# Two-layer hybrid block on one core: side-by-side copies of u, table loads placed by hand, transposes inside products, phi and key/value units exchanged

## The chip, the cores and the metric

The kernel runs on one core of one Trainium2 chip. The metric is the device time of one execution in microseconds. "Before" was run three times; one further execution was profiled, and every row below comes from that one.

## The reference

Two layers over 256 tokens of width 1024, in float32. Each layer is a feed-forward block, a token-mixing block of four mixers, a cross attention over 256 memory rows, and another feed-forward block, each with a norm in front and behind. Cut to what matters:

```python
for l in range(2):
    u = rmsnorm(h, ffn1_pre_g)
    h = h + 0.5 * rmsnorm((silu(u @ w_gate) * (u @ w_up)) @ w_down, ffn1_post_g)   # 2816 hidden
    u = rmsnorm(h, mix_pre_g)
    proj = u @ w_in                      # split into the inputs of four mixers
    y = [mla(...), nsa(...), fox(...), s5(...)]       # 4 heads of 64 each, s5: 16 groups, 64 states
    h = h + rmsnorm(group_rmsnorm(y) @ w_out, mix_post_g)
    u = rmsnorm(h, xa_pre_g); m = rmsnorm(mem, xa_mem_g)
    h = h + rmsnorm(cross_attention(u, m @ w_kv) @ w_o, xa_post_g)
    u = rmsnorm(h, ffn2_pre_g)
    h = h + 0.5 * rmsnorm(swiglu(u), ffn2_post_g)
```

s5 is a state-space recurrence over the tokens, computed in chunks of 4 tokens ("taps"). nsa attends to compressed blocks (phi is a two-layer map of key and value blocks), to selected blocks and to a window.

## The kernel before

**Units and slots.** All large weights come in units of 128 x 2048 float32 (1 MB), 98 per layer, in a fixed order. Unit u of a layer goes to slot (u + 98 l) mod 3. A slot has three buffers: raw (the DMA's target), w_hi and w_lo. `split` on ScalarE (L666) copies raw to w_hi in float32r in two halves; `split` on VectorE (L1144) writes w_lo = raw - w_hi, in two halves. ScalarE's split of a unit waits for its DMA and for unit_done of every earlier unit of the slot, since it overwrites w_hi. SyncE loads the next unit of a slot as soon as VectorE has split the last one. TensorE (PE) makes every large product three times: w_hi x_hi, w_lo x_hi, w_hi x_lo. The four phi units of a layer are the exception: PE reads them raw, they are never split, and the next load of the slot waits for PE instead.

**Order.** Each engine runs a list written out by hand and executes it in order; semaphores join the lists. PE waits in its own order, so whatever stands behind a waiting product waits too.

**Feed-forward.** 11 chunks of 256 hidden columns. `gate_up` (L1777) makes the products of one chunk for token halves t = 0 and 1 (units a and b), with the transposes of the chunk before in between; `ffn_down` follows. The first chunk, `gate_up_first` (L1802), also transposes the rows of h (`rows_of`), which ScalarE and VectorE turn into x_hi and x_lo (`fill_hi_of`, `fill_lo_of`, counted in x_split). On ScalarE the first block of a layer has two loops, chunks 2 to 4 and chunks 5 to 9; between them stand an Exp, an Abs and four Sin for the state-space tables, after which GpSimd builds these tables. In the first layer chunk 1 also holds the transposes of the scaled memory rows (`mem_transposed`, L1824), which ScalarE copies out and stores.

**Mixing.** Middle units m = 0 to 31: eight for w_in, then twelve, 8 to 19, of which 11, 13, 16, 18 are phi units and the others key/value units (KV0 to KV7) of the cross attention, then four for the output projection (20 to 23), four for queries and four for the cross attention's output. Middle unit m lies in slot m mod 3 in layer 0. PE's list from the selected-block attention (group 1) to the window attention (group 2), shortened:

```python
phi_unit(2); kv_half(6, 0); probs_transposed(1); kv_half(6, 1); phi_unit(3)
kv_half(7, 0); times_values(1)           # L2161
... # phi_t
kv_half(7, 1)                            # L2169
pe.wait_ge(*E.at("att_out", 3))
scores(2)                                # L2171
```

VectorE has `split_mid(21)`, `attention_out(1)` one behind the other (L1539, L1540), and ScalarE has `split_mid(21)`, the tanh of phi, `evac_kv(7)`, `split_mid(22)` (L1038 to L1043). The attention groups run in the order 0, 3, 1, 2; att_out 3 is the end of attention_out(1).

**State space.** u of the mixer is scaled in bank 5 of PSUM (s5_us), then copied to s_u with a rotation of its 32-partition blocks: sixteen copies of 32 x 128, eight by ScalarE (taps j = 0, 1), then eight by VectorE (taps 2, 3).

Of the kernel before, what the change touches and what calls it, by code (L numbers as in the profile page):

```python
# [9 lines left out]
ACT = mybir.ActivationFunctionType  # L10
# [6 lines left out]
KT = D // P  # L17
# [12 lines left out]
CH = 4  # L30
# [13 lines left out]

PHI_UNITS = [N_IN + i for i in (3, 5, 8, 10)]
KV_UNITS = [N_IN + i for i in (0, 1, 2, 4, 6, 7, 9, 11)]
KV_BANK = [0] + 7 * [1]
# [79 lines left out]
def program(nc, x, memory, weights, cols, mats, post, consts, out, mem_scratch):  # L127
# [5 lines left out]
    with ctx:  # L133
# [526 lines left out]
        def _(act):  # L660
            a = nc.scalar

            for l in range(DEPTH):
# [91 lines left out]
                def ffn_first(f):  # L755

                    if l == 0 and f == 0:
                        fill_hi_of(3 * f, 1, range(6))
                        split(*ffn_unit(l, f, "a", 1))
                        tanh_of(f, 0, 0)  # L760
                        fill_hi_of(3 * f, 1, (6, 7))
                        h_square(3 * f, 1)
                        load_gain(3 * f)
                        split(*ffn_unit(l, f, "b", 1))
                        tanh_of(f, 0, 1)
                        act.wait_ge(s_mem, 16)
                        for t in range(TT):
                            i = a.activation((mix_out, qk_a)[t][:, 0:D], mem3[:, t], ACT.Square, accum_out=ss[N_QM][:, t:t + 1])
                        i.then_inc(b_ss, 1)
                    else:  # L770
                        split(*ffn_unit(l, f, "a", 1))
                        fill_hi_of(3 * f, 1, range(6))
                        h_square(3 * f, 1)
                        load_gain(3 * f)
                        tanh_of(f, 0, 0)
                        fill_hi_of(3 * f, 1, (6, 7))
                        split(*ffn_unit(l, f, "b", 1))
                        tanh_of(f, 0, 1)
# [49 lines left out]
                a.activation(zone[:, 3072:3584], proj[:, 40:552], ACT.Sin, scale=-1.0, bias=quarter)  # L828
                a.activation(zone[:, 3584:4096], nsa_q[:, 40:552], ACT.Sin).then_inc(sem["trig_done"], 1)
                with act.Fori(FU // 2, FU - 1) as i:  # L830
                    ffn_piece(0, i, False)
                    act.wait_ge(s_con, 16)
# [40 lines left out]
                u_to = v3(s_u.rearrange("p g q -> p (g q)"), "p (i a q) -> p a i q", i=2, a=4)  # L873
                for j in range(2):
                    for q in range(4):
                        i = a.activation(u_to[32 * j:32 * j + 32, q], u_ps[32 * q:32 * q + 32, :, :, CH - 1 - j],
                                         ACT.Copy)
                i.then_inc(sem["proj_done"], 1)

                split_mid(4)  # L880
                evac(0, 1)
                split_mid(3)
                act.wait_ge(*E.at("s5_t", 1))
# [123 lines left out]
                evac_kv(1)  # L1007
                split_mid(12)
                act.wait_ge(*E.at("fox_cum", 1))
                for hh in range(H):  # L1010
# [12 lines left out]
                evac_kv(4)  # L1023
                split_mid(17)
                act.wait_ge(*E.at("nsa_t", 2))
                a.activation(nsa_q[0:HD, :], bank(6, 2)[0:HD], ACT.Copy).then_inc(sem["nsa_tc_act"], 1)
                evac_kv(5)
                attention(1)

                attention_t(1)  # L1030
                split_mid(19)
                evac_kv(6)
# [99 lines left out]
        def _(dve):  # L1132
            v = nc.vector

            for l in range(DEPTH):
# [120 lines left out]
                def ffn_first(f):  # L1256

                    fill_lo_of(E.at, 3 * f, 1, range(6))
                    split(*ffn_unit(l, f, "a", 1))
                    fill_lo_of(E.at, 3 * f, 1, (6, 7))  # L1260
                    gate_of(f, 0, 0)
# [42 lines left out]
                tt(u_in, u_in, row_r2, ALU.mult).then_inc(sem["s5_us"], 1)  # L1304
                dve.wait_ge(*E.at("proj_done", 2))
                u_ps = v3(bank(5), "p (i q r) -> p i q r", i=2, r=CH)
                u_to = v3(s_u.rearrange("p g q -> p (g q)"), "p (i a q) -> p a i q", i=2, a=4)
                for j in (2, 3):
                    for q in range(4):
                        i = v.tensor_copy(u_to[32 * j:32 * j + 32, q], u_ps[32 * q:32 * q + 32, :, :, CH - 1 - j])  # L1310
                i.then_inc(sem["s5_u_dve"], 1)
                dve.wait_ge(*E.at("s5_k", 1))
                tt(k_ps[:, :, 0:C2], k_ps[:, :, 0:C2], v3(pmat[:, W_D:W_D + PAIRS * C2], "p (g c) -> p g c",
                                                                g=PAIRS), ALU.add).then_inc(sem["s5_kd"], 1)
                split_mid(4)
                split_mid(3)
                dve.wait_ge(*E.at("s5_t", 1))
# [205 lines left out]
                attention_out(3)  # L1523
                split_mid(17)
                attention_max(1)

                attention_copy(1)
                split_mid(19)
                s, n, _ = mid(l, PHI_UNITS[3])
# [120 lines left out]
        def _(pe):  # L1650
# [4 lines left out]
            for l in range(DEPTH):  # L1655
# [91 lines left out]

                def gate_up_tile(f, unit, half, t, fill=None):

# [3 lines left out]
                    if not by_piece:  # L1753
                        pe.wait_ge(*E.at(split_done[s], ns + 1))
                    for k in range(KT // 2):
                        if by_piece and half == 0:
                            pe.wait_ge(*E.at(split_done[s], k - 2))
                        elif by_piece and k % 2 == 0:
                            pe.wait_ge(*E.at(split_done[s], k // 2))
# [17 lines left out]
                def gate_up(f, i):  # L1777

                    (a_, an, ans), (b_, bn, bns) = (ffn_unit(l, f, r, i) for r in ("a", "b"))
                    for t in range(TT):  # L1780
                        pe.wait_ge(*E.at("hid_done", i * 2 + (2 * f * FU + t - 1)))
                        o = gate_up_tile(f, (a_, an, ans), 0, t)
                        if t == 1:
                            o.then_inc(sem[unit_done[a_]], 1)
                        o = gate_up_tile(f, (b_, bn, bns), 1, t)
                        if t == 0:
                            o.then_inc(sem["gu_half"], 1)
                            hid_transposed(f, i - 1)
                            if l == 0 and f == 0 and isinstance(i, int) and i == 1:
                                mem_transposed()  # L1790
                    o.then_inc(sem[unit_done[b_]], 1)
# [10 lines left out]
                def gate_up_first(f):  # L1802
# [7 lines left out]
                    rows_of(p, 0, range(6, KT))  # L1810
                    gate_up_tile(f, b_, 1, 0, fill).then_inc(sem["gu_half"], 1)
                    rows_of(p, 1, range(6))
                    pe.wait_ge(*E.at("hid_done", 2 * f * FU))
                    gate_up_tile(f, a_, 0, 1, fill).then_inc(sem[unit_done[a_[0]]], 1)
                    rows_of(p, 1, range(6, KT))
                    gate_up_tile(f, b_, 1, 1, fill).then_inc(sem[unit_done[b_[0]]], 1)
# [97 lines left out]
                pe.wait_ge(*E.at("row_scale_kept", 1))  # L1914
                pe.wait_ge(s_con, 16)
                pe.wait_ge(*E.at("s5_u_dve", 1))
                for q in range(2):
# [493 lines left out]
```

## Time and profile before

| | us |
|---|---|
| three runs | 1291.06, 1292.61, 1293.25 |
| median | 1292.61 |
| profiled execution | 1290.97 |
| its span, first to last instruction | 1289.1 |
| PE busy | 1260.7 |
| VectorE busy | 820.6 |
| ScalarE busy | 668.1 |
| GpSimd busy | 236.5 |

Busy is the time in which an engine has an instruction in work. Matmuls are pipelined and their ends are modelled, so a row of PE shows when a product starts, and its drawn end overlaps the next one. The idle time in brackets counts from the drawn end. A line number can be a helper's: L1659 is every matmul, L1139 every tensor-tensor operation of VectorE. DVE is VectorE, ACT is ScalarE, POOL is GpSimd, SP is SyncE.

### The profile page before, as it was taken

What the parts mean: (1) busy time and instruction counts of PE and PEld (TensorE: products, weight loads), DVE (VectorE), ACT (ScalarE), POOL (GpSimd) and SP (SyncE); (2) the same over time, 40 slices, a digit from 0 to 9 for tenths busy, and PEclk for the clock granted to TensorE, in tenths of its full rate; (3) what the DMA queues carried; (4) which work ended last, traced back from release to release, by engine and by line L of the source; (5) the groups of instructions that cost most, each with busy time, mean ns of one, the idle gap of its engine ahead of it and who ended that gap; (6) DMA issues with size and microseconds to landing.
All of it is one profiled execution on the core that took longest, in us unless ns stands there. A gap on an engine that the chain in (4) does not pass through costs nothing.

```text
span 1289.1 us, 18528 instructions
## 1 busy us (share of the span) xinstructions
PE 1260.7 (98%) x6836; PEld 1072.6 (83%) x6836; DVE 820.6 (64%) x1155; ACT 668.1 (52%) x1091; POOL 236.5 (18%) x251
## 2 busy tenths in 40 slices
PE   7999999999999999999999999999999999999998
PEld 5888788899988878888878878888998798788886
DVE  5657956775557565555576587667856565755554
ACT  6455546574536564444464545564745455644442
POOL 1618911000002010000045297000000010100000
PEclk9999999999999999999999999999999999999999
DMA  9754554334525356555455555533245243655551
GB/s 342 256 189 153 191 195 148 135 125 146 199 84 184 127 209 220 177 184 193 164 183 193 195 176 183 180 147 140 105 164 205 90 174 128 232 179 186 176 187 65
DMA packets 32442, 222.65 MB, mean 173 GB/s; under 512 B 3584, under 2 KB 4096, under 8 KB 6784
## 3 DMA queue, kind: packets, MB, share of 16 engines
q1 hardware_dynamic: 30080, 209.28, 45.0%
q10 hardware_dynamic: 2304, 12.58, 2.6%
q8 instruction: 38, 0.62, 0.2%
q14 instruction: 20, 0.16, 0.0%
HBM read 219.75 MB, written 2.10 MB: 172 GB/s over the span
## 4 chain that ended last, share of the span: by engine, by line
PE 88%; DVE 5%; issue 3%; ACT 2%; DMA 1%; POOL 1%; SPq 0%; DVEq 0%; ACTq 0%; POOLq 0%
PE PS L1659 83%; DVE w_lo L1139 3%; PE PS L1774 1%; DMA raw<-in_weights 1%; PE PS L1988 1%; DVE x_lo L1142 1%; ACT w_hi L671 1%; DVE rope_t L1310 0%; ACT x_hi L719 0%; DVE work L1142 0%; DVE h L1142 0%; PE PS L1800 0%; PE PS L2241 0%; PE PS L1972 0%; PE PS L2032 0%
## 5 line engine op out<-in xcount | busy, mean ns | idle before, releaser
L1139 DVE TENSOR_TENSOR w_lo<-raw,w_hi 128x1024 fp32r<-128x1024 f32 (+1 forms) x378 | 484.0, 1323 | 221.2 <-ACT w_hi L671 217.7
L671 ACT ACTIVATE w_hi<-raw 128x1024 fp32r<-128x1024 f32 x368 | 368.9, 1053 | 207.8 <-PE PS L1659 203.0
L1659 PE MATMUL PS<-w_hi,x_hi 128*128 128x512 f32 (+2 forms) x1104 | 425.4, 385 | 13.5 <-DVE w_lo L1139 7.0
L1659 PE MATMUL PS<-w_lo,x_hi 128*128 128x512 f32 (+2 forms) x1104 | 413.5, 375 | 0.0
L1659 PE MATMUL PS<-w_hi,x_lo 128*128 128x512 f32 (+2 forms) x1104 | 407.7, 375 | 0.0
L1659 PEld LDWEIGHTS PS<-w_hi,x_hi 128*128 128x128 f32 x1104 | 208.3, 189 | 58.0 <-issue 10.6
L1659 PEld LDWEIGHTS PS<-w_hi,x_lo 128*128 128x128 f32 x1104 | 208.1, 189 | 38.2
L1659 PEld LDWEIGHTS PS<-w_lo,x_hi 128*128 128x128 f32 x1104 | 208.5, 189 | 34.8 <-issue 0.5
L521 POOL TENSOR_SCALAR st<-st 128x1 f32<-128x1 f32 x32 | 20.3, 634 | 619.8 <-ACT proj L694 550.8
L1659 PE MATMUL PS<-w_hi,hid_hi 128*128 128x512 f32 x336 | 131.5, 391 | 0.0
L1659 PE MATMUL PS<-w_lo,hid_hi 128*128 128x512 f32 x336 | 130.8, 389 | 0.0
L732 ACT ACTIVATE work<-PS,st 128x256 f32<-128x256 f32 x88 | 41.9, 476 | 149.1 <-PE PS L1659 147.5
L1659 PE MATMUL PS<-w_hi,hid_lo 128*128 128x512 f32 x336 | 103.5, 389 | 0.0
L1659 PE MATMUL PS<-x_hi,w_hi 128*128 128x256 f32 x288 | 84.2, 292 | 1.0 <-DVE x_lo L1142 0.9
L1142 DVE SCALAR_TENSOR_TENSOR work<-work,PS 128x256 f32<-128x256 f32 x88 | 36.5, 414 | 71.5 <-ACT work L732 71.5
L1659 PE MATMUL PS<-x_lo,w_hi 128*128 128x256 f32 x288 | 81.4, 283 | 0.0
L1659 PE MATMUL PS<-x_hi,w_lo 128*128 128x256 f32 x288 | 81.3, 282 | 0.0
L1659 PEld LDWEIGHTS PS<-w_hi,hid_lo 128*128 128x128 f32 x336 | 63.1, 188 | 13.2
L1659 PEld LDWEIGHTS PS<-w_lo,hid_hi 128*128 128x128 f32 x336 | 63.1, 188 | 12.8
L1659 PEld LDWEIGHTS PS<-w_hi,hid_hi 128*128 128x128 f32 x336 | 63.1, 188 | 12.8
L1659 PEld LDWEIGHTS PS<-x_hi,w_hi 128*128 128x128 f32 x288 | 55.0, 191 | 3.2 <-issue 2.7
L1659 PEld LDWEIGHTS PS<-x_lo,w_hi 128*128 128x128 f32 x288 | 55.1, 191 | 0.1
(274 smaller groups left out, 1334.5 us busy)
## 6 DMA issues: line engine op xcount, KB each, us to landing
raw<-in_weights SPq DMA_DIRECT2D x194, 1024.0 KB, 4.8
pmat<-in_mats ACTq DMA_DIRECT2D x3, 1664.0 KB, 7.8
gain<-in_post ACTq DMA_DIRECT2D x8, 512.0 KB, 3.7
zone<-mem_scratch ACTq DMA_DIRECT2D x2, 1024.0 KB, 5.7
raw<-in_weights SPq DMA_DIRECT2D x3, 512.0 KB, 7.3
h<-in_x SPq DMA_DIRECT2D x2, 512.0 KB, 6.2
zone<-in_mem SPq DMA_DIRECT2D x1, 1024.0 KB, 11.1
mem_scratch<-zone ACTq DMA_DIRECT2D x1, 1024.0 KB, 9.0
```

The costliest lines, as they stand in the source:

```text
L521: E.step(g.tensor_scalar(o, a, s1, s2, op0, op1))
L671: a.activation(w_hi[s][:, c_], raw[s][:, c_], ACT.Copy).then_inc(sem[hi_done[s]], 1)
L732: a.activation(f_th[:, t], bank(4 + t)[:, 0:UC], ACT.Tanh, scale=rstd[n][:, t:t + 1]).then_inc(sem["tanh_done"], 1)
L1139: return v.tensor_tensor(o, x_, y_, op)
L1142: return v.scalar_tensor_tensor(out=o, in0=x_, scalar=s_, in1=y_, op0=op0, op1=op1)
L1659: return t_.matmul(o, a_, b_, start=first, stop=last)
L1774: o = t_.transpose(bank(6)[:, j * S + t * P:j * S + (t + 1) * P], f_hid[:, t, j * P:(j + 1) * P], ident)
L1988: i = t_.transpose(bank(b)[:, hh * P:(hh + 1) * P], probs[:, at:at + P], ident)
```

## The change

- Phi and key/value units are exchanged in the load order: units 16 and 18 become KV6 and KV7, 17 and 19 phi 2 and phi 3. PE's list stays. The splits of 17 and 19 become 16 and 18, and split(18) goes ahead of attention_t(1).
- In the opening of a feed-forward block the x tiles 6 and 7 of token half 1 are filled earlier on ScalarE, in the first opening of all on VectorE too. On PE the row transposes of token half 1 stand inside the products of units a and b, not between them.
- mem_transposed moves twelve products further down in chunk 1, behind unit a's products of token half 1.
- A Tanh on one column stands ahead of ScalarE's second loop, an Exp on one column behind split(12). They place the table loads.
- Both engines copy u at the same time: ScalarE the blocks q = 0, 1 for all four taps, VectorE q = 2, 3. Units 3 and 4 are split in this order.

```diff
-PHI_UNITS = [N_IN + i for i in (3, 5, 8, 10)]
-KV_UNITS = [N_IN + i for i in (0, 1, 2, 4, 6, 7, 9, 11)]
+PHI_UNITS = [N_IN + i for i in (3, 5, 9, 11)]
+KV_UNITS = [N_IN + i for i in (0, 1, 2, 4, 6, 7, 8, 10)]
...
@@ -756,9 +756,9 @@
                         fill_hi_of(3 * f, 1, range(6))
+                        fill_hi_of(3 * f, 1, (6, 7))
                         split(*ffn_unit(l, f, "a", 1))
                         tanh_of(f, 0, 0)
-                        fill_hi_of(3 * f, 1, (6, 7))
...
@@ -827,6 +827,7 @@
                 a.activation(zone[:, 3584:4096], nsa_q[:, 40:552], ACT.Sin).then_inc(sem["trig_done"], 1)
+                a.activation(st[:, 0:1], ident[:, 0:1], ACT.Tanh)
                 with act.Fori(FU // 2, FU - 1) as i:
...
-                for j in range(2):
-                    for q in range(4):
+                for q in range(2):
+                    for j in range(CH):
                         i = a.activation(u_to[32 * j:32 * j + 32, q], u_ps[32 * q:32 * q + 32, :, :, CH - 1 - j],
                                          ACT.Copy)
                 i.then_inc(sem["proj_done"], 1)
+                split_mid(3)
+                evac(0, 1)
                 split_mid(4)
-                evac(0, 1)
-                split_mid(3)
...
                 split_mid(12)
+                a.activation(st[:, 0:1], ident[:, 0:1], ACT.Exp)
                 act.wait_ge(*E.at("fox_cum", 1))
...
-                split_mid(17)
+                split_mid(16)
...
                 attention(1)
+                split_mid(18)
                 attention_t(1)
-                split_mid(19)
                 evac_kv(6)
...
@@ -1256,8 +1258,12 @@
-                    split(*ffn_unit(l, f, "a", 1))
-                    fill_lo_of(E.at, 3 * f, 1, (6, 7))
+                    if l == 0 and f == 0:
+                        fill_lo_of(E.at, 3 * f, 1, (6, 7))
+                        split(*ffn_unit(l, f, "a", 1))
+                    else:
+                        split(*ffn_unit(l, f, "a", 1))
+                        fill_lo_of(E.at, 3 * f, 1, (6, 7))
...
-                dve.wait_ge(*E.at("proj_done", 2))
+                dve.wait_ge(*E.at("s5_us", 1))
-                for j in (2, 3):
-                    for q in range(4):
+                for q in (2, 3):
+                    for j in range(CH):
...
+                split_mid(3)
                 split_mid(4)
-                split_mid(3)
...
-                split_mid(17)
+                split_mid(16)
                 attention_max(1)
+                split_mid(18)
                 attention_copy(1)
-                split_mid(19)
...
@@ -1753,6 +1759,8 @@
                     for k in range(KT // 2):
+                        if between and k == KT // 4:
+                            between()
...
                         if t == 1:
                             o.then_inc(sem[unit_done[a_]], 1)
+                            if l == 0 and f == 0 and isinstance(i, int) and i == 1:
+                                mem_transposed()
                         o = gate_up_tile(f, (b_, bn, bns), 1, t)
                         if t == 0:
                             o.then_inc(sem["gu_half"], 1)
                             hid_transposed(f, i - 1)
-                            if l == 0 and f == 0 and isinstance(i, int) and i == 1:
-                                mem_transposed()
...
-                    gate_up_tile(f, b_, 1, 0, fill).then_inc(sem["gu_half"], 1)
-                    rows_of(p, 1, range(6))
+                    def next_rows():
+                        pe.wait_ge(*E.at("x_split", FILL[fill] + KT))
+                        rows_of(p, 1, range(6))
+
+                    gate_up_tile(f, b_, 1, 0, fill, next_rows).then_inc(sem["gu_half"], 1)
                     pe.wait_ge(*E.at("hid_done", 2 * f * FU))
-                    gate_up_tile(f, a_, 0, 1, fill).then_inc(sem[unit_done[a_[0]]], 1)
-                    rows_of(p, 1, range(6, KT))
+                    gate_up_tile(f, a_, 0, 1, fill, lambda: rows_of(p, 1, range(6, KT))).then_inc(sem[unit_done[a_[0]]], 1)
...
                 pe.wait_ge(*E.at("row_scale_kept", 1))
                 pe.wait_ge(s_con, 16)
+                pe.wait_ge(*E.at("proj_done", 2))
                 pe.wait_ge(*E.at("s5_u_dve", 1))
```

## Rows read from the trace of the kernel before

**Rows 1.** The page, part 1: busy time and share of the span, one engine.

```profile
PE 1260.7 (98%) x6836; PEld 1072.6 (83%) x6836; DVE 820.6 (64%) x1155; ACT 668.1 (52%) x1091; POOL 236.5 (18%) x251
```

**Rows 2.** The page, part 5: columns are instruction, busy, mean ns, idle before, releaser.

```profile
L1139 DVE TENSOR_TENSOR w_lo<-raw,w_hi 128x1024 fp32r<-128x1024 f32 (+1 forms) x378 | 484.0, 1323 | 221.2 <-ACT w_hi L671 217.7
...
L671 ACT ACTIVATE w_hi<-raw 128x1024 fp32r<-128x1024 f32 x368 | 368.9, 1053 | 207.8 <-PE PS L1659 203.0
```

**Rows 3.** Waits of PE: released line, releaser, us in total, times, longest.

```profile
PE PS L1723 <- DVE h L1142: 2.5, 2, 1.3
```

**Rows 4.** Timeline of the opening, ScalarE and PE: start, us, instruction, idle before.

```profile
19.59 2.01 ACT L671 ACTIVATE w_hi<-raw 128x1024 fp32r<-128x1024 f32 x2 [0.94 <-DMA raw<-in_weights]
...
23.36 0.50 PE L1659 MATMUL PS<-w_hi,x_hi 128*128 128x512 f32 x1 [0.85 <-DVE x_lo L1142]
...
32.05 1.20 PE L1829 MATMUL PS<-con,zone 128*128 128x128 f32 x9 [1.16 <-DVE zone L1269]
...
34.05 1.89 ACT L747 ACTIVATE zone<-PS 128x2048 f32<-128x2048 f32 x1 [1.77 <-PE PS L1829]
```

**Rows 5.** Timeline of the second feed-forward opening: ScalarE, VectorE, PE.

```profile
464.78 2.00 ACT L671 ACTIVATE w_hi<-raw 128x1024 fp32r<-128x1024 f32 x2
...
464.67 0.61 DVE L1142 SCALAR_TENSOR_TENSOR x_lo<-PS,pcol,x_hi 128x128 fp32r<-128x128 f32 x2 [0.42 <-ACT x_hi L719]
...
468.24 0.47 PE L1659 MATMUL PS<-w_hi,x_hi 128*128 128x512 f32 x1 [0.46 <-DVE x_lo L1142]
```

**Rows 6.** Timeline of the state-space start: ScalarE, VectorE, PE.

```profile
219.91 2.23 ACT L876 ACTIVATE rope_t<-PS 32x128 f32<-32x128 f32 x8 [2.84 <-DVE PS L1139]
...
222.17 2.41 DVE L1310 COPY rope_t<-PS 32x128 f32<-32x128 f32 x8 [2.30 <-ACT rope_t L876]
...
229.76 0.49 PE L1659 MATMUL PS<-w_hi,x_hi 128*128 128x496 f32 x1 [0.26 <-DVE w_lo L1139]
```

**Rows 7.** Timeline around the third group's exponentials: ScalarE, PE.

```profile
298.60 1.53 ACT L1011 ACTIVATE qk_a<-PS 1x256 f32<-1x256 f32 x4 [2.32 <-PE PS L1659]
...
316.80 1.28 ACT L935 ACT_TABLE_LOAD   x1
...
320.83 0.85 PE L1988 MATMUL PS<-con,zone 128*128 128x128 f32 x6 [0.62 <-ACT zone L938]
```

**Rows 8.** Timeline of the second loop, VectorE.

```profile
127.67 7.94 DVE L1139 TENSOR_TENSOR w_lo<-raw,w_hi 128x1024 fp32r<-128x1024 f32 x4
```

**Rows 9.** Chain in the second loop (start, us, what), and PE's row there.

```profile
120.80 1.07 ACT w_hi L671
...
132.44 0.50 PE L1659 MATMUL PS<-w_hi,x_hi 128*128 128x512 f32 x1 [0.80 <-DVE w_lo L1139]
```

**Rows 10.** Timeline around units 18 to 21: PE, ScalarE, VectorE, PE.

```profile
347.37 0.36 PE L1659 MATMUL PS<-w_hi,x_hi 128*128 128x256 f32 x1 [0.68 <-DVE w_lo L1139]
...
351.63 2.00 ACT L671 ACTIVATE w_hi<-raw 128x1024 fp32r<-128x1024 f32 x2 [1.21 <-DMA raw<-in_weights]
...
352.98 2.35 DVE L1139 TENSOR_TENSOR w_lo<-raw,w_hi 128x1024 fp32r<-128x1024 f32 x2
...
355.25 0.22 DVE L1445 TENSOR_SCALAR st<-PS 128x4 f32<-128x4 f32 x2
...
356.83 0.48 PE L1659 MATMUL PS<-nsa_k,nsa_q 64*128 64x256 f32 x1
```

**Rows 11.** Timeline of PE at the start.

```profile
8.72 0.76 PE L1659 MATMUL PS<-w_hi,x_hi 128*128 128x512 f32 x1 [2.32 <-DVE w_lo L1139]
...
12.67 0.39 PE L1659 MATMUL PS<-w_hi,x_hi 128*128 128x512 f32 x1
```

**Rows 12.** Windows at the end: bounds, length, busy by engine, PEclk, DMA share, GB/s.

```profile
1282.00:1284.00 2.00, 1.18 (x6) 0.64 (x4) 1.46 (x2) 1.23 (x4) 0.43 (x1) 1.00 0.00 0
...
1285.50:1286.00 0.50, 0.00 (x0) 0.00 (x0) 0.50 (x2) 0.00 (x0) 0.00 (x0) 0.80 0.96 393
...
1286.00:1289.00 3.00, 0.00 (x0) 0.00 (x0) 0.68 (x2) 0.00 (x0) 0.00 (x0) 0.50 0.47 175
```

More of the change, by code:

```diff
@@ L774, in ffn_first @@
                         load_gain(3 * f)
+                        fill_hi_of(3 * f, 1, (6, 7))
                         tanh_of(f, 0, 0)
-                        fill_hi_of(3 * f, 1, (6, 7))
                         split(*ffn_unit(l, f, "b", 1))
@@ L1746, in _, with gate_up_tile @@
                 hid_tiles = [(hid_hi[:, j * S:(j + 1) * S], hid_lo[:, j * S:(j + 1) * S]) for j in range(2)]
-                def gate_up_tile(f, unit, half, t, fill=None):
+                def gate_up_tile(f, unit, half, t, fill=None, between=None):
                     s, _, ns = unit
```

## Prediction

> **What bounds the kernel.** I read the page first. Its first part puts TensorE at 98% of the span [rows 1], and the chain of work that ended last runs through PE's three-pass products nearly all the way. So an edit gains only where PE waits, and costs only where it makes PE wait. VectorE and ScalarE have room on average, but each weight unit passes through both: two ScalarE halves of about 1.05 us and two VectorE halves of about 1.2 us [rows 2]. I then went through the timeline of PE for every place where one product starts later than the pace allows. A 512-column product starts every 0.23 us but is drawn 0.39 us long, a 256-column one every 0.12 and 0.28; so a wait costs the idle time in the bracket plus 0.16 us. The waits that the diff can touch, each read in the timeline of the engine that ends it, are few and short: they add up to some 15 us, a little over 1% of the time. After the start the longest is 1.3 us idle, in a line that the diff doesn't touch [rows 3]. A new wait of a few us would therefore weigh as much as everything that can be won.
>
> **The change, part by part.**
>
> Opening of the first feed-forward stage and the memory rows. PE waits 0.85 us for the last two x tiles of token half 1, because ScalarE and VectorE split unit a of chunk 1 first, at 19.59, the moment it lands; it waits 1.16 us for the scaled memory rows [rows 4]. With the 0.16 these are 1.01 and 1.32 us, and the first x tile of token half 1 costs another 0.55 us some 5 us earlier (0.39 idle, the pattern of rows 5). The first goes: rows 6 and 7 are transposed some 2 us sooner and filled before the split. The second goes: twelve products of 0.23 us (2.7 us) now stand in front of the memory transposes, and the ScalarE copy behind them (1.9 us [rows 4]) ends before twelve more products do. But something is late next: chunk 1 may start only when the gate of chunk 0 has emptied bank 4. That gate stands behind the split, which can't start before the landing, 19.5. Split and gate end about 24.0; PE would be there at 23.1. So 2.9 us of waits go and 0.9 us comes: gain 1.95 us, bounds 1.0 and 2.9.
>
> The other three openings (the rows of token half 1 inside the products). PE waits 0.46 us after the six transposes [rows 5], and 0.49 and 0.46 in the two others, so 0.62 each with the drawn end. Six products (1.36 us) now follow those transposes. The fill on ScalarE stands behind a split that ends at 466.8 in any case [rows 5], so the first x tile is complete at 467.6, when PE, after the same number of transposes and products, wants it. About 0.05 us each is left: gain 3 x 0.57 = 1.7 us, bounds 1.0 and 1.9. The new wait for all eight x tiles of half 0 costs nothing: the last is written at 465.3 [rows 5], the products reach it at 465.6.
>
> Copies of u. ScalarE takes 2.23 us for its eight copies and VectorE only then 2.41 us for its own [rows 6]; VectorE's splits of two units follow, unit 4 ahead of unit 3, and PE waits 0.26 us for unit 3 [rows 6], 0.42 by start times. Side by side the copies end at about 222.2. Unit 3's slot is free at about 225.1, whoever copies (PE's last products on unit 0 end then); with unit 3 first it is ready at 228.5, before PE wants it at 229.3. The next thing late is the copy of the tap tables behind unit 4's split, ending about 232.1 on VectorE, which is when PE arrives. Gain 0.4 x 2 layers = 0.8 us, bounds 0 and 0.85. That both engines read one bank at once may slow the copies; 2.8 us of slack hide it.
>
> Exp table. The load of 1.28 us stands directly ahead of the third group's exponentials, and PE waits 0.62 us for their end [rows 7], 0.78 by start times. After the split of unit 12 ScalarE is idle for 2.32 us before fox_cum [rows 7], so the load is hidden there, and the exponentials begin 0.9 us sooner. Gain 0.78 x 2 = 1.55 us, bounds 1.2 and 1.6.
>
> Table loads out of the second loop. Four loads of 1.28 us per layer, each as in [rows 7], leave ScalarE. The PE waits nearest to them are 0.96 us (0.80 idle, at 132.44 [rows 9]) and 0.78 us (17.7 us later) per layer. But those are VectorE's: the chain runs from PE's release at 120.80 over w_hi [rows 9] straight into VectorE's w_lo, whose four halves from 127.67 take 7.94 us with no idle time in front [rows 8], 2.0 each where 1.2 is usual, while GpSimd works on large state-space tables. The table load is not in this chain. I take nothing; bounds 0 and 3.4 us.
>
> Units exchanged. Before, unit 19 (KV7, slot 1) could only be loaded once phi unit 2 was used up; its split comes late and PE waits 0.68 us [rows 10], about 1.0 by start times. Now KV7 is unit 18 in slot 0; its raw data is there early, its split goes ahead of attention_t(1), and this wait is gone: gain 0.95 us per layer (the evacuation of bank 1 by ScalarE is what PE then meets).
> The price is one unit later. Slot 0 next takes unit 21, an output-projection unit. A phi unit is used raw and never occupies w_hi; KV7 does. split(21) starts at 351.63 now, released by its DMA alone [rows 10], since slot 0's last user, phi unit 3, is long done. After the change ScalarE must wait with it for the end of kv_half(7,1). That lies just behind 356.83, the start of the next product [rows 10]; 0.95 us sooner it is about 355.95. VectorE has the same split in its queue directly ahead of attention_out(1), and the PE instruction right behind kv_half(7,1) is scores(2), which waits for that attention_out [rows 10]. Step by step: ScalarE half 1.1, two VectorE halves 2.4, the six operations of attention_out(1) 1.45 (from 355.25 [rows 10] to 356.7), the semaphore 0.13: scores(2) starts at 360.9. Before the change PE passes here without a wait; it would now be ready at 355.85. That is a new wait of 5.05 us. Nothing covers it: PE executes in order, and the phi tail, mixer transposes and output rows are all behind scores(2). ScalarE and VectorE later keep their old distances to scores(2), so nothing is given back. Bounds 3.6 (should attention_out overlap) and 5.3. Net of the exchange: 10.1 - 1.9 = +8.2 us.
>
> Sum without the clock: -1.95 - 1.7 - 0.8 - 1.55 + 8.2 = +2.2 us.
>
> The clock. At the start nine 512-column products run at 0.44 us each, from 8.72 to 12.67; from there they stand 0.23 apart [rows 11]. That is the step from 1.2 to 2.4 GHz, and the slow stretch cost 9 x 0.21 = 1.9 us. At the end PE's last product ends at 1283.2; the granted clock is still 1.00 until 1285.5, 0.80 in the next half us and 0.50 after [rows 12]. So there 2.6 us of rest were enough to bring it down. The new wait is twice that. I expect it to fall in each layer and PE to work on at half pace for a while; bounds per layer 0 and 1.9 us, and because part of the slow stretch may lie in the wait itself I take 1.65, together +3.3 us.
> The Trainium skill (TensorE: Matmul & The Clock Gate, Part 1) says that an idle PE is gated back to the lower clock and gets the full one only after sustained work; the rows at both ends of this trace agree, and by that rule the sum is +5.5 us, without it +2.2.
>
> Total: +2.2 + 3.3 = +5.5 us. The profiled execution took 1290.97 us (span 1289.1 and 1.9 around it), which gives 1296.5. The median of the three runs is 1292.61, 1.64 above, so I add this: **1298 us**.
>
> **Rivals.**
> 1. The new wait without the clock: 1292.6 + 2.2 = 1294.8. For it: no wait now in the kernel brings the clock down, the longest included [rows 3]. Against: the end of the trace [rows 12]. 0.15.
> 2. The other side: the exchange does not block. Should VectorE finish the attention output before PE needs it, or the split chain be largely covered, the 7.9 us of removed waits stay: 1292.6 - 7.9 = 1284.7 with no new wait. It decides at 4.0 us of new wait per layer with the clock held (2.3 with it lost): below that the kernel is faster. Against it: queue order and slot arithmetic are fixed, and the chain's durations are all measured. 0.10.
> 3. The table loads do carry the loop's waits: 3.4 us more gain, 1294.6. For it: they stand in the same iterations. Against: VectorE has no idle time in front of the waiting product. 0.07.
> 4. More is lost: the early reordering pays nothing, a clock loss costs the full 1.9 or more, the feed-forward openings meet new waits: 1300 to 1303. 0.08.
> The forecast has 0.60.
>
> **How the numbers follow.** A difference under 0.2% (2.6 us) can't be told from none. Range: forecast with its bounds 1295 to 1300.5; rivals 1 and 3 at 1294.7 come in with their spread, rival 2 stays out: 1292.5 to 1301. Faster (below 1290.0) 0.12: rival 2 and a bit of 3. Same 0.23: rivals 1 and 3 for the most part, and the low edge of the forecast. Slower 0.65.
>
> **What would show it.** In the profile after, PE stands before the first scores product of the window group (nsa_k, nsa_q) in both layers for 5 us, released by VectorE's mix_out; w_hi of that unit starts right after the last product of kv_half(7,1), not on a DMA. The granted clock of the 10 us after each of these waits is under 1.00, and 512-column products there are 0.43 apart. ScalarE has no table load inside the loop, yet the PE waits near 132 and 150 are still there. The waits at 320.8, 347.4, 229.8 and 468.2 are gone. It is wrong if scores(2) starts within 2 us of kv_half(7,1), or if the loop waits vanish with the table loads.

## The result, and the profile after

The change made the kernel slower: 1303.85 us median of four runs (1302.3 to 1305.04) against 1291.84 of four runs of before beside them (1290.84 to 1293.25), a ratio of 1.009 with a 95% interval of 1.0074 to 1.0106. I had forecast 1298, in a range of 1292.5 to 1301: the direction was right, the size was not. The profiled execution after the change has a span of 1301.2 us, before 1289.1, so 12.1 us have to be found.

The page after, part 1, one row. PE has as many instructions as before and is drawn busy for 6.8 us longer [rows 1]: it does the same work more slowly somewhere.

```profile
PE 1267.5 (97%) x6836; PEld 1078.9 (83%) x6836; DVE 824.4 (63%) x1155; ACT 658.9 (51%) x1087; POOL 239.2 (18%) x251
```

Waits of PE after: released line, releaser, us in total, times, longest.

```profile
PE PS L1665 <- DVE mix_out L1141: 9.8, 2, 4.9
PE PS L1665 <- DVE w_lo L1141: 6.5, 5, 3.8
PE PS L1665 <- DVE x_lo L1144: 4.8, 11, 0.6
```

The first row is new: two waits of 4.9 us, one in each layer, on the attention output. Of the longest waits no other grew, except that the longest on w_lo is now 3.8 us; that one is the first, at the start (below). Here is that place in the first layer, in the timeline of the kernel after, one engine behind the other: ScalarE, VectorE, PE (start, us, instruction, idle before).

```profile
354.16 2.00 ACT L671 ACTIVATE w_hi<-raw 128x1024 fp32r<-128x1024 f32 x2 [5.79 <-PE PS L1665]
...
355.25 2.36 DVE L1141 TENSOR_TENSOR w_lo<-raw,w_hi 128x1024 fp32r<-128x1024 f32 x2 [4.25 <-ACT w_hi L671]
357.53 0.22 DVE L1451 TENSOR_SCALAR st<-PS 128x4 f32<-128x4 f32 x2
...
358.22 0.76 DVE L1141 TENSOR_TENSOR mix_out<-PS,st 128x256 f32<-128x256 f32 x2
...
353.84 0.28 PE L1665 MATMUL PS<-w_hi,x_lo 128*128 128x256 f32 x1
359.03 1.22 PE L1665 MATMUL PS<-nsa_k,nsa_q 64*128 64x256 f32 x2 [4.91 <-DVE mix_out L1141]
```

This is the chain I had worked out: PE finishes kv_half(7,1) (last product at 353.84), only then does ScalarE start w_hi of unit 21. Its bracket names PE, where before it named the DMA [rows 10]. VectorE's halves of unit 21 follow, then attention_out(1), then scores(2). By start times the wait is 359.03 - 353.84 - 0.12 = 5.07 us (forecast 5.05). In the second layer scores(2) starts at 1000.34, again with 4.91 us idle.

What I had too small comes next. Windows of the kernel after: bounds, length, busy by engine, then the granted clock (PEclk), DMA share, GB/s.

```profile
354.00:357.60 3.60, 0.12 (x2) 0.00 (x0) 2.35 (x4) 2.00 (x2) 0.00 (x0) 1.00 0.00 0
357.60:367.84 10.24, 8.81 (x34) 7.50 (x35) 7.93 (x20) 4.06 (x9) 0.00 (x0) 0.50 0.55 190
367.84:372.00 4.16, 4.16 (x27) 3.44 (x25) 1.64 (x5) 3.02 (x10) 0.00 (x0) 1.00 0.10 39
999.30:1009.54 10.24, 9.20 (x35) 7.77 (x36) 7.98 (x17) 4.45 (x10) 0.00 (x0) 0.50 0.59 205
```

The clock falls to 0.50 (1.2 GHz) inside the wait, 1.4 us before scores(2), and stays there for 10.24 us, of which PE works 8.8. To price it, take the distance from scores(2) to the transpose of h that ends PE's wait for VectorE's h; both ends are rows. After the change they are these.

```profile
402.95 1.29 PE L1729 MATMUL PS<-con,h 128*128 128x128 f32 x8 [1.24 <-DVE h L1144]
...
1044.46 1.51 PE L1729 MATMUL PS<-con,h 128*128 128x128 f32 x10 [1.24 <-DVE h L1144]
```

The distance is 402.95 - 359.03 = 43.92 us and 1044.46 - 1000.34 = 44.12 us. Before, the first was 396.71 - 356.83 = 39.88 [rows 10]. These are the rows of before that end it, and both ends in the second layer.

```profile
396.71 0.96 PE L1723 MATMUL PS<-con,h 128*128 128x128 f32 x5 [1.28 <-DVE h L1142]
...
991.93 2.88 PE L1659 MATMUL PS<-nsa_k,nsa_q 64*128 64x256 f32 x16
...
1031.76 1.51 PE L1723 MATMUL PS<-con,h 128*128 128x128 f32 x10 [1.27 <-DVE h L1142]
```

The second layer's distance was 39.83. So the slow stretches cost 4.04 and 4.29 us, 8.3 us in all, where I had put 3.3.

The smaller edits, in the timeline after: PE at the start, the loop (VectorE, PE), the copies of u and the next wait of PE, the Exp's table load.

```profile
10.01 0.77 PE L1665 MATMUL PS<-w_hi,x_hi 128*128 128x512 f32 x1 [3.79 <-DVE w_lo L1141]
...
12.71 0.47 PE L1665 MATMUL PS<-w_hi,x_hi 128*128 128x512 f32 x1
...
25.05 0.50 PE L1665 MATMUL PS<-w_hi,x_hi 128*128 128x512 f32 x1 [0.69 <-DVE work L1144]
...
126.68 7.93 DVE L1141 TENSOR_TENSOR w_lo<-raw,w_hi 128x1024 fp32r<-128x1024 f32 x4
...
131.43 0.50 PE L1665 MATMUL PS<-w_hi,x_hi 128*128 128x512 f32 x1 [0.76 <-DVE w_lo L1141]
...
218.90 2.22 ACT L877 ACTIVATE rope_t<-PS 32x128 f32<-32x128 f32 x8 [2.85 <-DVE PS L1141]
...
218.90 2.42 DVE L1316 COPY rope_t<-PS 32x128 f32<-32x128 f32 x8
...
230.78 0.39 PE L1665 MATMUL PS<-w_hi,x_lo 128*128 128x496 f32 x1
231.22 0.63 PE L1665 MATMUL PS<-rope_t,zone 128*128 128x64 f32 x4
...
295.03 1.28 ACT L1010 ACT_TABLE_LOAD   x1
```

The gate of chunk 0 is what PE meets at 25.05, 0.85 us by start times (forecast 0.9). The table load now runs at 295.03, ahead of its use. The copies of u start together, and neither engine is slowed by it although both read one bank: 2.22 and 2.42 us for eight copies, 2.23 and 2.41 before [rows 6]. The wait in the loop is still there at 131.43, with no table load near it. The start itself was 1.3 us later in this execution (first product 10.01, before 8.72 [rows 11]); ScalarE's first split there starts when the DMA of the first weights lands, at 8.55 (7.26 before), which the diff doesn't touch.

### The profile page after: what moved, and what is told of

It reads as the page before. It is cut to its first block, busy times and chain, and to the rows that moved or that the text cites. A ratio compares the mean times of both kernels' runs of the same rounds, so it can differ in the third digit from the quotient of the medians.

```text
span 1301.2 us, 18571 instructions
## 1 busy us (share of the span) xinstructions
PE 1267.5 (97%) x6836; PEld 1078.9 (83%) x6836; DVE 824.4 (63%) x1155; ACT 658.9 (51%) x1087; POOL 239.2 (18%) x251
## 4 chain that ended last, share of the span: by engine, by line
PE 91%; DVE 4%; issue 2%; ACT 1%; DMA 1%; POOL 0%; SPq 0%; ACTq 0%; DVEq 0%; POOLq 0%
PE PS L1665 86%; DVE w_lo L1141 2%; PE PS L1782 1%; PE PS L1999 1%; DVE x_lo L1144 1%; DMA raw<-in_weights 1%; ACT w_hi L671 1%; PE PS L1808 1%; DVE work L1144 0%; DVE h L1144 0%; PE PS L2050 0%; DVE mix_out L1141 0%; ACT x_hi L719 0%; PE PS L1983 0%; PE PS L1930 0%
```

## The experiments

Each ratio is against before, run beside it on the same chip: 1291.13 us for the first four, again 1291.13 on another chip for the next four, 1291.26 on a third for the last two. Between these groups, and against the 1303.85 above, the ratios compare better than the times.

**The exchange, undone and alone.** First the changed kernel without the exchange:

```diff
-PHI_UNITS = [N_IN + i for i in (3, 5, 9, 11)]
-KV_UNITS = [N_IN + i for i in (0, 1, 2, 4, 6, 7, 8, 10)]
+PHI_UNITS = [N_IN + i for i in (3, 5, 8, 10)]
+KV_UNITS = [N_IN + i for i in (0, 1, 2, 4, 6, 7, 9, 11)]
...
-                split_mid(16)
+                split_mid(17)
...
-                split_mid(18)
                 attention_t(1)
+                split_mid(19)
```

> The changed kernel with the exchange of the units alone undone. Theory A (the exchange puts a 5.07 us wait and about 4.3 us of half-pace work in each layer and takes away a wait of 0.95 us): 1303.85 - 2 x (5.07 + 4.3 - 0.95) = 1287.0, so faster than before by the 4.8 us of the other edits; granted clock 1.00 from 13 us to the end; no wait before scores(2). Rival B (the exchange costs its 4.1 us per layer and the other edits lose the rest, for instance through the table loads or the copies of u): 1295 to 1297.

Measured: 1285.61 us (ten runs, 1285.09 to 1288.01), ratio 0.9955 (0.9942 to 0.9969). The wait before scores(2) is gone; the old one on KV7's split is back, as this row of its timeline shows:

```profile
344.81 0.36 PE L1665 MATMUL PS<-w_hi,x_hi 128*128 128x256 f32 x1 [0.68 <-DVE w_lo L1141]
```

Then the opposite: before with these lines of the exchange alone.

> The kernel before with the exchange alone. Theory A: 1291.84 + 2 x (5.07 + 4.3 - 0.95) = 1308.7, slower than the full change; a wait of 5 us before scores(2) in each layer, the granted clock at 0.50 for about 10 us around it. Rival B: 1300 or less, with less slow clock.

Measured: 1309.09 us (1307.94 to 1312.2), ratio 1.0131 (1.0095 to 1.0167). Its wait before scores(2) is the same, 4.91 us idle in each layer. Its windows show the slow stretch, in the first layer still longer than in the kernel after:

```profile
359.24:372.89 13.65, 11.88 (x41) 9.90 (x42) 9.90 (x23) 7.08 (x18) 0.00 (x0) 0.50 0.45 155
...
1004.36:1014.60 10.24, 8.57 (x33) 7.37 (x34) 7.96 (x18) 3.82 (x9) 0.00 (x0) 0.50 0.51 182
```

From scores(2) to the transpose of h this run took 45.45 us in the first layer (361.01 to 406.46), against the 39.88 of before: the longer stretch cost 5.6. In the whole time the exchange costs 18 us either way (1303.85 - 1285.61 and 1309.09 - 1291.13), and everything else in the diff together gains 5.5 (1291.13 - 1285.61). The whole loss lies in the exchange.

**Where the wait goes if only VectorE's order is mended.** The changed kernel, VectorE's list:

```diff
-                split_mid(21)
                 attention_out(1)
+                split_mid(21)
                 dve.wait_ge(*E.at("phi_t", 1))
```

> The changed kernel, exchange kept, with attention_out(1) ahead of split(21) in VectorE's list. Theory A (the wait is nothing but the queue order on VectorE): the wait before scores(2) is gone, the clock stays at 1.00, and the 0.95 us per layer of the exchange are kept: 1303.85 - 2 x (5.07 + 4.3) = 1285.1. Rival B (split(21) is needed soon after by the output rows, so that the wait only moves down the list): a wait of 2 to 4 us before out_rows(1,0), 1290 to 1296.

Measured: 1293.1 us (1291.98 to 1296.27), ratio 1.001 (0.9995 to 1.0024): the rival by its time, but the wait stands elsewhere than it said. In its timeline, VectorE, ScalarE, PE:

```profile
354.87 2.36 DVE L1141 TENSOR_TENSOR w_lo<-raw,w_hi 128x1024 fp32r<-128x1024 f32 x2 [2.96 <-ACT w_hi L671]
357.15 0.21 DVE L1141 TENSOR_TENSOR small<-PS,pcol 128x60 f32<-128x60 f32 x1
...
358.14 0.25 ACT L1042 ACTIVATE small<-small 128x60 f32<-128x60 f32 x1 [2.42 <-DVE small L1141]
...
358.70 0.40 PE L1665 MATMUL PS<-small,pmat 128*64 128x15 f32 x4 [2.21 <-DVE small L1144]
```

The first operation of phi now stands behind the split, and PE waits 2.4 us one step later, for phi, not before the output rows. Even this shorter wait brings the clock down (windows of the same run):

```profile
359.11:362.52 3.41, 3.41 (x15) 2.99 (x16) 2.67 (x3) 3.27 (x8) 0.00 (x0) 0.50 0.63 267
...
993.99:1000.82 6.83, 6.12 (x24) 5.21 (x25) 5.27 (x8) 4.46 (x10) 0.00 (x0) 0.50 0.66 215
```

**The clock by itself.** Wait and clock come together, so I took them apart: the wait stays, and PE multiplies the identity by constants in it, into a half bank that nobody uses. `keep_clock` is a helper that both kernels already have; they call it with two products ahead of row transposes. The edit, in the changed kernel (22, 11 or 6 products):

```diff
                 kv_half(7, 1)
+                keep_clock(7, 22)
                 pe.wait_ge(*E.at("att_out", 3))
                 scores(2)
```

> The changed kernel with 22 products of 256 float32 columns that nobody reads put on PE between kv_half(7,1) and the wait for att_out 3: 4.8 us of work inside the 5.07 us wait. Theory A (rest brings the clock down, and that is 4.3 us per layer of the loss): scores(2) starts when it did, the granted clock stays at 1.00, 1303.85 - 8.6 = 1295.2. Rival B (the small float32 products behind the wait are slow for another reason, the clock record is a by-product): no change, 1303.9.

Measured: 1303.01 us (1302.07 to 1303.32). It tells nothing by its time, since the filler was twice as long as meant: each of its 256-column float32 products is two PE instructions. Its timeline:

```profile
353.24 9.66 PE L1665 MATMUL PS<-con 128*128 128x256 f32 x44
362.83 1.35 PE L1665 MATMUL PS<-nsa_k,nsa_q 64*128 64x256 f32 x6
```

The filler outlasts the wait by 4.5 us per layer (362.83 - 353.24 - 5.07), about what the clock had cost. With half of it:

> The changed kernel with eleven 256-column float32 products on the identity behind kv_half(7,1), into an unused half bank: 22 PE instructions of 0.22 us, 4.8 us, which fit into the 5.07 us wait before scores(2). They compute nothing that is used. Theory A (the fall of the clock costs 4.1 to 4.3 us per layer on top of the wait): the granted clock stays 1.00 from 350 to 372 us, scores(2) starts where it did, and the time is 1303.8 - 2 x 4.2 = about 1295.5. Rival B (the slow stretch after the wait is not what costs, the products would be held up by something else): 1303 to 1304.

Measured: 1294.93 us (six runs, 1293.74 to 1297.31), ratio 1.0033 (1.0021 to 1.0044). Its timeline and windows:

```profile
353.06 4.91 PE L1665 MATMUL PS<-con 128*128 128x256 f32 x22
358.13 2.88 PE L1665 MATMUL PS<-nsa_k,nsa_q 64*128 64x256 f32 x16 [0.16 <-DVE mix_out L1141]
```

```profile
358.10:363.00 4.90, 4.87 (x35) 4.31 (x36) 3.26 (x7) 3.58 (x8) 0.00 (x0) 1.00 0.50 201
```

scores(2) starts just as late, 5.07 us after the filler's first instruction; the sixteen products of it take 2.88 us and the clock is 1.00. The distance to the transpose of h is back at 398.09 - 358.13 = 39.96 us:

```profile
398.09 1.50 PE L1729 MATMUL PS<-con,h 128*128 128x128 f32 x10 [1.26 <-DVE h L1144]
```

So the price of the clock in the time of the whole kernel is 7.4 us by the two ratios, 8.3 by the distances above and 8.9 by the two medians (1303.85 - 1294.93), which come from different chips. Last, six products, so that part of the wait remains:

> As the run with eleven filler products, but with six: 12 PE instructions, 2.6 us, and then some 2.4 us without work before scores(2). Theory A (the clock falls after such a rest too, and then stays low for several us, as it did behind the 2.37 us wait of the run with attention_out(1) first): granted clock 0.50 for 3 to 10 us in each layer, time 1297 to 1302. Rival B (a rest of 2.4 us is too short here): clock 1.00, about 1295.5 as with eleven.

Measured: 1301.51 us (1300.33 to 1306.43), ratio 1.0091 (1.0073 to 1.0108). PE rests 2.48 us by start times before scores(2), and the clock falls all the same (windows of this run, both layers):

```profile
359.28:366.10 6.82, 6.82 (x29) 5.80 (x29) 5.26 (x8) 3.87 (x9) 0.00 (x0) 0.50 0.49 168
...
1000.98:1007.80 6.82, 6.82 (x28) 5.59 (x27) 6.38 (x10) 4.02 (x11) 0.00 (x0) 0.50 0.48 173
```

Here the fall comes 0.9 us after scores(2) has begun, in the second layer 2.3 us after, so all 6.8 us of each are worked through. This row ends the distance in the first layer:

```profile
401.40 1.51 PE L1729 MATMUL PS<-con,h 128*128 128x128 f32 x10 [1.27 <-DVE h L1144]
```

The distances from scores(2) are 43.06 us (358.34 to 401.40) and 42.97 (998.66 to 1041.63), so the clock still costs some 3.1 us per layer, 6.2 of 8.3 in all. A rest of half the length saved 2.1 us; the ratio, 1.0091 against 1.009 for the kernel after, does not tell it from nothing.

**A better order under the exchange.** Unit 22's slot was last used by a phi unit and is free early; unit 21's is not. So the changed kernel with the two splits exchanged, in the lists of both engines:

```diff
-                split_mid(21)
+                split_mid(22)
...
-                split_mid(22)
+                split_mid(21)
```

> The changed kernel with split_mid(21) and split_mid(22) exchanged in the lists of both ScalarE and VectorE; the exchange of units stays. Unit 22's slot was last used by phi unit 3 and is free early; unit 21's is free only after kv_half(7,1). Theory A (the whole loss is the order of these two splits): no wait before scores(2), none before the phi products, granted clock 1.00 there, and the two waits that the exchange removed (1.05 us per layer) stay gone: 1285.6, the version without the exchange, less about 2 us, 1283.5 to 1285. Rival B (split(21) is late for the output rows instead, or unit 22 lands too late): a wait of 1 us or more before the output rows or again before scores(2), 1287 to 1296.

Measured: 1286.85 us (eight runs, 1285.55 to 1291.93), ratio 0.9972 (0.9958 to 0.9985). The 5 us are gone, but not all of the wait (timeline, VectorE and PE):

```profile
350.19 2.35 DVE L1141 TENSOR_TENSOR w_lo<-raw,w_hi 128x1024 fp32r<-128x1024 f32 x2
352.46 0.22 DVE L1451 TENSOR_SCALAR st<-PS 128x4 f32<-128x4 f32 x2
...
353.96 2.88 PE L1665 MATMUL PS<-nsa_k,nsa_q 64*128 64x256 f32 x16 [0.57 <-DVE mix_out L1141]
```

Unit 22 lands at 348.7 and its split still stands in front of attention_out(1), so that PE waits 0.73 us by start times. The gain on the other side is smaller than the 1.05 us that I had expected. From the products of phi unit 3 to scores(2) PE takes 11.14 us here (342.82 to 353.96) and 11.21 without the exchange (343.06 to 354.27), in the second layer 11.15 and 11.22: in this order the exchange gives 0.07 us per layer, next to nothing. I then put attention_out(1) ahead of split(22) on VectorE:

> The kernel with the splits of 21 and 22 exchanged, and attention_out(1) ahead of split(22) on VectorE. In the profile of the run without this step the six operations of attention_out(1) stand behind split(22) on VectorE and end at 353.91, where PE is ready 0.73 us earlier. Theory A: without the split in front they end at about 351.8, the wait of 0.73 us before scores(2) goes in both layers, and split(22), now ending 1.4 us later at about 354, delays phi's operations by 0.2 us, which PE doesn't feel: span 1283.7 - 1.45 = about 1282.3. Rival B (the wait moves to the phi products, as it did when this step was made with split(21)): span 1283 to 1288, with a wait before the small/pmat products.

Measured: 1287.7 us (1286.94 to 1292.03), ratio 0.9974 (0.9963 to 0.9986): no gain. scores(2) has no wait any more, but it turned up some 10 us later, at the output rows, where neither theory had it. PE's timeline and two windows of this run:

```profile
364.17 0.70 PE L1665 MATMUL PS<-w_hi,x_hi 128*128 128x512 f32 x1 [0.71 <-DVE x_lo L1144]
```

```profile
295.96:299.38 3.42, 3.42 (x18) 3.42 (x18) 1.86 (x4) 1.50 (x4) 0.72 (x1) 0.50 0.00 0
...
364.23:367.64 3.41, 3.41 (x8) 2.65 (x9) 1.39 (x6) 1.83 (x7) 0.00 (x0) 0.50 0.66 279
```

Splits 22 and 21 now end later on VectorE, and x_lo for the output rows with them. The wait is there in the second layer too (998.59, 0.71 us idle). The second window is a fall of the clock right at this wait, and 999.11 to 1002.52 is another, at the same wait of the second layer. The first has no wait in front of it at all. The kernel without this step has no such fall in its profiled execution (mean clock 1.000 against 0.995), so the profiled spans, 1283.7 and 1287.6, don't compare the two orders; the ratios do.

**The loop.** The kernel with the two splits exchanged, but without the Tanh:

```diff
-                a.activation(st[:, 0:1], ident[:, 0:1], ACT.Tanh)
                 with act.Fori(FU // 2, FU - 1) as i:
```

> The kernel with the two splits exchanged, but without the Tanh ahead of ScalarE's second loop, so that the four table loads per layer are back in the loop. Theory A (the waits near 132 and 150 us are VectorE's, slowed while GpSimd works): no change against the kernel with the Tanh, within 1 us. Rival B (the table loads carry part of these waits): 1 to 3.4 us slower.

Measured: 1287.25 us (1284.54 to 1289.06), ratio 0.9963 (0.9945 to 0.9981), against 1286.85 with it on the same chip: no difference that can be told, though with these intervals one of 1 us can't be excluded. The trace is sharper: it has the table loads in the loop again, and the waits of PE as they were (0.78 and 0.61 us idle, 0.76 and 0.61 with the Tanh):

```profile
127.49 1.28 ACT L671 ACT_TABLE_LOAD   x1 [3.13 <-PE PS L1664]
...
130.89 0.50 PE L1664 MATMUL PS<-w_hi,x_hi 128*128 128x512 f32 x1 [0.78 <-DVE w_lo L1140]
```

Then the other suspect, GpSimd, with its large operations thinned (eight of twelve; one shown):

```diff
-                tt(tc5, ciw, over_c(aij, J5, 0), ALU.mult)
+                tt(tc5[:, :, 0:1], ciw[:, :, 0:1], over_c(aij, J5, 0)[:, :, 0:1], ALU.mult)
```

> The kernel with the splits of 21 and 22 exchanged, and eight of the twelve large GpSimd operations of the state-space tables (128 x 1280 and 128 x 1024) cut to their first tap, a fifth and a quarter of their size; the tables beyond it are left out. The order of every engine and ScalarE's lists stay. Theory A (VectorE's w_lo halves, 2.0 us each instead of 1.2 while GpSimd works, make PE wait near 131 and 148 us): GpSimd is done by about 120, the halves behind that take 1.2 us, both waits go in both layers: span 1283.7 - 2 x (0.92 + 0.77) = about 1280.3. Rival B (something else in the loop, ScalarE's order or the DMA): both waits stay, span 1283 to 1284.

Measured: 1284.0 us (four runs, 1281.48 to 1285.75), ratio 0.9936 (0.9921 to 0.9952), with the tables' later taps left out. Neither wait is in the loop any more, in either layer. The place shows in VectorE's timeline of this run; the second row shows the four halves that took 7.93 us above:

```profile
119.78 3.32 DVE L1144 TENSOR_TENSOR w_lo<-raw,w_hi 128x1024 fp32r<-128x1024 f32 x2 [2.25 <-ACT w_hi L674]
...
123.86 7.83 DVE L1144 TENSOR_TENSOR w_lo<-raw,w_hi 128x1024 fp32r<-128x1024 f32 x4
```

The pair of halves from 119.78 took 3.32 us instead of 5.00, and that was enough. I had expected GpSimd to be done by 120; it was not, and the next four halves are nearly as slow as ever. From the first product to the same product of the mixer, near 200 us, this execution took 193.59 us (8.41 to 202.00) and the one with full tables 195.33 (9.12 to 204.45): 1.74 less, where the two waits were 0.92 + 0.77. The span of the profiled execution is nevertheless 1284.0 us, the number of the rival, where 1280.3 was forecast. The clock accounts for it: it fell twice in the second layer, with no wait in front of either (windows of this run).

```profile
923.89:930.72 6.83, 6.83 (x34) 6.83 (x34) 3.01 (x6) 1.95 (x6) 0.72 (x1) 0.50 0.11 43
995.57:998.98 3.41, 3.41 (x9) 2.65 (x9) 0.74 (x4) 1.20 (x5) 0.00 (x0) 0.50 0.47 199
```

PE worked through these 10.24 us, so by half pace about 5.1 were lost. The fastest of the four runs, with a mean clock of 0.999, had a span of 1279.6.

## Why the prediction was off, point by point

- **The wait from the exchange: right.** Place, releaser and length are as worked out (5.07 us in each layer, forecast 5.05), and the wait on KV7 is gone. (Without the exchange scores(2) starts 0.20 us behind the last product, not 0.12; counted from there the wait is 4.99.) The gain on KV7 was read too high: from phi unit 3's products to the next attention products PE took 4.69 us before (345.62 to 350.31) and takes 3.98 after (343.55 to 347.53), so 0.71 us per layer went, near the 0.68 idle of [rows 10], where I had made "about 1.0 by start times" of it and forecast 0.95. Undoing the exchange and doing it alone both confirm that nothing else made the kernel slower. The match is closer than the working: the steps as listed (355.95 + 1.1 + 2.4 + 1.45 + 0.13) end at 361.03, not 360.9, and would have given a wait of 5.18.
- **The clock: the step that failed.** That it would fall was right. The term "1.65 per layer, bounds 0 and 1.9" was mis-sized: it measured 4.04 and 4.29. I had priced it by the slow stretch at the start of the kernel, 1.9 us lost over nine products [rows 11], and took that for the upper end. Behind the waits it stayed at 0.50 for 10.24 us. At half pace PE loses half of the time that it works in the stretch: of 8.8 and 9.2 us worked this makes 4.4 and 4.6, near the measured 4.04 and 4.29. How long PE works before the clock returns behind a wait in mid-kernel is in no row of before; the 1.9 was therefore no bound. With 8.3 us in place of 3.3, 5.0 are missing here, most of the 5.85 between 1298 and 1303.85. That the wait is the cause is shown: with eleven filler products in it the clock stayed at 1.00 and the distance was 39.96 us again.
- **The Trainium skill's rule** (TensorE: Matmul & The Clock Gate, Part 1), that an idle PE is gated back and needs sustained work for the full clock, stood on the right side: the windows above agree, with 0.50 from inside the 5.07 us wait on and 1.00 again 10.24 us later.
- **Openings and memory rows: right.** From the first product to the loop's first wait were 123.72 us before [rows 9, 11], and are 121.42 after (10.01 to 131.43), 2.3 less. Of this 0.6 is the clock of the start: six products at half pace instead of nine. That leaves 1.7 (forecast 1.95), with the new wait at the gate at 0.85 as expected. In the three other openings the waits behind the row transposes (468.24 in [rows 5]) are gone, 0.6 us each.
- **Exp: right.** No wait before the exponentials' transposes is left in PE's list of waits.
- **Copies of u: half.** Unit 3's wait of 0.42 us is gone, but 0.22 remains at 231.22, in front of the tap tables' products (230.78 to 231.22 where 0.22 is the pace). So the gain is 0.2 us per layer, not 0.4; I had named this as the next thing late and put it 0.2 us too early. The four smaller edits were not run one by one; their gains are read from the timelines, and together they are 5.5 us where 6.0 was forecast.
- **Table loads: right.** They carry nothing of the loop's waits; GpSimd's work beside VectorE does. Both were shown by runs.
- **The sum.** Without the clock I had +2.2 us. The span grew by 12.1, of which 1.3 is the later start and 8.3 the clock; 2.5 is left.
- **Rivals.** Rival 1, the wait without the clock, is refuted by the windows at 0.50; its argument, that no wait of before brings the clock down, rested on waits of at most 1.3 us idle. "The exchange does not block" is refuted. Rival 4, more lost, had the right ingredient and a chance of 0.08, but ended at 1303 with a clock loss of 1.9 or little more.

Of the kernels that compute everything the fastest is the changed one without the exchange, 1285.61 us, 0.45% under before. The exchange in a better order ends beside it (0.9972 against 0.9955, overlapping intervals).

## What to carry to other kernels

Before units change places in a ring of buffers, ask for each what the next user of the same buffer waits for: a unit that is read raw frees its converted copy early, one that is converted does not. A wait of some us on TensorE has a second price, the work done at half pace behind it: here 4.0 and 4.3 us behind waits of 5.07. If the wait can't be removed, filler products in it give that part back, provided that they fill it and don't outlast it. When a wait goes at one place, look at which instruction inherits the delay: here it went to phi once, and to the output rows once.

## What was not expected of the hardware

- After a wait of 5.07 us the clock stood at 0.50 for 10.24 us in three of four cases and for 13.65 in one, counted from inside the wait. After waits of 2.4 to 2.5 us it stood there for 3.41 us once and for 6.83 three times. The four cases with 5.07 us are two kernels, the four others two more, one profiled execution each.
- Falls without a wait in front appear in two profiled executions. At 295.96 (3.41 us, attention_out(1) first) and, in the second layer, at 923.89 (6.83 us, thinned tables) PE had just run products of 65 and 1 columns, 128-column transposes and, in the first case, products of 4 columns. At 995.57 (3.41 us, thinned tables) it had run sixteen products of 15 columns and stood at the same place at which the other execution fell behind a wait of 0.87 us; so that this wait brought the clock down there is not shown. In the profiled executions of before, of the kernel without the exchange and of the one with the splits exchanged the clock is at 1.00 in all these places.
- The spread between runs of one kernel goes with their mean clock. Of 48 executions of before that ran beside the experiments (a 49th took 2557.8 us at a mean clock of 1.000, unexplained), the 37 with a mean clock of 0.998 or more took 1290.5 to 1293.3 us, the eight with 0.997 took 1291.1 to 1294.2, the three with 0.994 or 0.995 took 1295.9 to 1298.0. Where the clock fell in the slow ones can't be told, as they have no trace.
- A float32 product of 256 columns (identity by constants, the filler) is two instructions of 0.22 us each on PE, 0.44 us together.
